# A weight stream of an expert stage: which entries are fetched aside, and where the shared expert stands

## The chip, the cores and the metric

The kernel runs on one core of a Trainium2 chip. The metric is the device time of one execution in microseconds, as the median of several runs. The core has five engines with queues of their own: TensorE (PE; matmuls, and weight loads as PEld), VectorE (DVE), ScalarE (ACT), GpSimd (POOL) and SyncE (SP), which here does nothing but issue transfers from device memory (HBM) into the on-chip memory and wait for their places to come free.

## The reference

Two transformer blocks run over 256 tokens of width 1024, in float32. The change touches the second half of the first block, a mixture of experts in four groups of eight, of which each token takes one group and in it two experts, with one shared expert for all tokens:

```python
def hier_moe(h, ...):
    t = h.reshape(-1, d)
    # combine: (tokens, 32) weights of the chosen experts, else 0
    ...
    a = jnp.einsum('nd,edf->nef', t, w_gate)       # w_gate, w_up: (32, 1024, 256)
    b = jnp.einsum('nd,edf->nef', t, w_up)
    hid = jax.nn.silu(a) * b * combine[:, :, None]
    routed = jnp.einsum('nef,efd->nd', hid, w_down)     # w_down: (32, 256, 1024)
    shared = (jax.nn.silu(t @ w_sh_gate) * (t @ w_sh_up)) @ w_sh_down
    return (routed + shared).reshape(bsz, slen, d)
```

Before it come a norm, an attention and convolution mixer with its output projection, and another norm. After it comes the second block: pooling, windowed attention, an output projection and a dense feed-forward part.

## The kernel before

**The stream.** All large weights lie in one array, `stream`, as entries of 128 x 2048 float32 (1024 KB each). SyncE fetches them in the order in which TensorE uses them. There are 14 entries for the mixer (0 to 13), then group 0 (entries 14 to 37), the shared expert's gate, up and down matrices (38, 39, 40), group 1 (41 to 64), group 2 (65 to 88), group 3 (89 to 112), and then the second block. (`entry_at` turns this order of use into the order in the array.) A group has `PAIRS` = 2 halves of four experts, and a half has 12 entries: eight for gate and up (`gate_up`), and four for down (`down`).

**Places.** An entry's place is as a rule one of the `SLOTS` = 8 places of `ring`, used in turn. Seven entries, those from `ASIDE_AT` = 20 to 26, are fetched aside instead, into room that stands empty at that time: five into the end of `work` (free when attention and convolution are done), and two into `turned_w` (free when the mixer's output projection is done). `ring_number(n)` is an entry's number among the ring's own, so entry 27 is number 20. With eight ring places and seven aside, fifteen entries, 14 to 28, can be on the chip before the expert stage has used any.

**Giving places back.** TensorE raises the semaphore `used` once for each entry it has passed, ring or aside. The raise hangs on the first matmul of a later step: the next entry's, the transposes of the hidden activations after the eighth gate and up entry, or `scatter`. SyncE's queue is strictly in order. For a ring entry it works out `gone`, the entry that held the place before, and waits for `used` to reach `gone + 1`; what is queued behind that wait waits too. Since 20 to 26 free no ring place, entry 34 takes the place of 19 and entry 35 that of 27:

```python
gone = ring_number(n) - SLOTS
if gone >= ASIDE_AT:
    gone += ASIDE
```

**The expert stage on TensorE.** `moe_group` gathers up to 32 tokens for each expert of the group by matmuls with a selection matrix (32 matmul records of 128x128 by 128x256), then for each half runs `gate_up`, `turn_hidden` (behind ScalarE's silu and VectorE's product), and `down`. The results of a half are scattered back into four PSUM banks by `scatter`: for half 0 that is after the second entry of half 1's `gate_up`, for half 1 at the group's end. Matmuls of an expert use 32 columns of the array, and four experts' run beside one another. An entry is eight matmul records. Groups 0 to 2 are written out, group 3 is the body of a loop which the data may repeat; here it ran once.

**The shared expert** runs after group 0, over all 256 tokens: `shared_gate_up` (64 matmul records of 128x128 by 128x256 over two entries), ScalarE's silu and VectorE's product (`shared_silu`, `shared_hidden`), `shared_turned` (four transposes and a copy), and `shared_down` (16 records of 128x128 by 128x512 with one entry), which adds to the same PSUM banks as `scatter`. Its down entry is given back by the first gather matmul of group 1 (`after_shared`).

The steps' lines are helpers' lines in the profile: nearly all matmuls carry line 1320, and are told apart by what they read.

Of the kernel before, what the change touches and what calls it, by code (L numbers as in the profile page):

```python
# [24 lines left out]
P = 128  # L25
D = 1024
DT = D // P
TOK = 256
# [32 lines left out]
B1 = 17  # L61
# [7 lines left out]
MOE_AT = B1 - 3  # L69
SHARED_AT = MOE_AT + MOE_GROUP  # L70
ASIDE_AT, ASIDE, ASIDE_WORK = 20, 7, 5
ASIDE_FROM = WORK - ASIDE_WORK * SLOT
# [43 lines left out]
def two_blocks(nc, x, meta, consts, small, gains, positions, stream, out):  # L116
    ctx = ExitStack()
    with ctx:
# [176 lines left out]
        def is_aside(n):  # L295
            return ASIDE_AT <= n < ASIDE_AT + ASIDE

        def ring_number(n):

            return n if n < ASIDE_AT else n - ASIDE  # L300

        def home(n):

            if not is_aside(n):
                return ring[:, ring_number(n) % SLOTS, :]
            i = n - ASIDE_AT
            if i < ASIDE_WORK:
                return work[:, ASIDE_FROM + i * SLOT:ASIDE_FROM + (i + 1) * SLOT]
            return turned_w[:, (i - ASIDE_WORK) * SLOT:(i - ASIDE_WORK + 1) * SLOT]

        def slot_ready(eng, n):

            if is_aside(n):
                eng.wait_ge(full2[n - ASIDE_AT], 16)
            else:
                eng.wait_ge(full[ring_number(n) % SLOTS], 16 * (ring_number(n) // SLOTS + 1))
# [117 lines left out]
        def _(sp):  # L434
# [3 lines left out]
            sp.dma_start(vec[:], small).then_inc(const_in, 16)  # L438
            for n in range(B1 + LOOPED * MOE_GROUP):
                if is_aside(n):  # L440

                    if n == ASIDE_AT:
                        sp.wait_ge(s["o_ps"], 2 * HEADS)
                        sp.wait_ge(s["convg_done"], CT)
                    if n == ASIDE_AT + ASIDE_WORK:
                        sp.wait_ge(s["mix_ps"], 2 * NT)
                    sp.dma_start(home(n), stream[entry_at(n)]).then_inc(full2[n - ASIDE_AT], 16)
                    continue
                gone = ring_number(n) - SLOTS
                if gone >= ASIDE_AT:  # L450
                    gone += ASIDE
                if 0 <= gone < Q_SLOT:
# [34 lines left out]
        def _(act):  # L487
# [178 lines left out]
            for g in range(LOOPED):  # L666
                moe_group(g)
                if g == 0:
                    shared_silu()
# [193 lines left out]
        def _(dve):  # L863
# [336 lines left out]
            for g in range(LOOPED):  # L1200
                moe_group(g, rankp[:, :, g * PER_GROUP:(g + 1) * PER_GROUP],
                          rankp[:, :, (g + 1) * PER_GROUP:(g + 2) * PER_GROUP], g == 0)
                if g == 0:
                    shared_hidden()
# [113 lines left out]
        def _(pe):  # L1318
# [292 lines left out]
            def shared_down():  # L1611
                slot_ready(pe, SHARED_AT + 2)
                pe.wait_ge(s["hst_sb"], 1)
                for i in range(NT):
                    for n in range(2):
                        for f in range(2):
                            last = mm(ps[:, 2 * i + n, :], hs[:, f, i * P:(i + 1) * P],
                                      home(SHARED_AT + 2)[:, f * D + n * 512:f * D + (n + 1) * 512], False, False,
                                      skip_group_check=True)

            def moe_group(it, g, moe_slot, freed, first=False, after_shared=False):

# [4 lines left out]
                for t in range(DT):  # L1627
                    for i in range(NT):
                        begin = mm(ps[:, gather_bank(t), (t % 2) * TOK:(t % 2 + 1) * TOK], xh[:, i, t * P:(t + 1) * P],
                                   sel[:, i, :], t % 2 == i == 0, False, skip_group_check=True)  # L1630
                        if after_shared and t == i == 0:
                            begin.then_inc(freed, 1)
                if first:
# [87 lines left out]

            def first_slot(k):

                slot_ready(pe, MOE_AT + k)
                return home(MOE_AT + k)

# [8 lines left out]
            for g in range(LOOPED):  # L1735
                moe_group(g, g, moe_slot(g) if g else first_slot, used, g == 0, g == 1)
                if g == 0:
                    shared_gate_up()
# [317 lines left out]
```

## Time and profile before

| | |
|---|---|
| median of 3 runs | 743.07 us (741.06 to 743.9) |
| the profiled execution's own time | 743.77 us |
| its span, first to last instruction | 741.9 us |
| granted TensorE clock, mean | 0.947 of full |
| PE busy | 662.8 us (89% of the span) |
| DVE, ACT, POOL busy | 334.6, 280.4, 42.9 us |
| read from HBM | 180.48 MB, 245 GB/s over the span |

The page cuts the span into 40 slices of 18.5 us. Of these, slices 7 to 20 hold the first block's end and the expert stage. Times in all rows are microseconds from the start of the span. In a timeline a row gives the start, the duration, the engine, the line, the operation, what is written and read, the count of records merged into it, and in brackets how long the engine stood idle just before and what ended that. A busy time alone says little: whether TensorE or the stream sets the pace differs between stages, so stretches are read one at a time.

### The profile page before, as it was taken

The page shows a single profiled execution, that of the slowest core. Times are in us where ns is not written, and L with a number is a line of the kernel's source. Part 1 is how long each engine was busy: PE and PEld are TensorE (multiplying, and loading weights), DVE is VectorE, ACT ScalarE, POOL GpSimd, SP SyncE. Part 2 cuts the span into 40 slices and gives each one's busy share as a digit, 9 for nine tenths or more (in the row PEclk, how much of TensorE's full clock was granted, in tenths as well). Part 3 has the DMA queues.
Part 4 walks back from the last instruction along what each step waited for, and adds up shares of the span by engine and source line. Part 5 has one row for each costly group of instructions (what it writes and reads, how often), then busy time and mean ns, then how long its engine had stood idle before and what let it go on. Part 6 is the DMA issues. An engine that isn't in the chain of part 4 may idle for free.

```text
span 741.9 us, 10752 instructions
## 1 busy us (share of the span) xinstructions
PE 662.8 (89%) x4431; PEld 516.6 (70%) x4431; DVE 334.6 (45%) x606; ACT 280.4 (38%) x521; POOL 42.9 (6%) x63
## 2 busy tenths in 40 slices
PE   8999899997895777677678999999989999999996
PEld 5979787733641133042148999989789999999994
DVE  7677555621020102012057565638845554445554
ACT  6655562311010110011045565673545433344432
POOL 1000102000000000000026400000000000000000
PEclk9999999999999687698799999999999999999998
DMA  9925309589869999999995534335525545545201
GB/s 354 417 90 223 114 1 407 245 340 388 348 251 424 420 422 421 422 419 422 420 420 208 197 114 148 137 115 174 187 106 204 182 173 197 198 170 180 105 1 57
DMA packets 26144, 182.22 MB, mean 246 GB/s; under 512 B 3040, under 2 KB 3168, under 8 KB 4464
## 3 DMA queue, kind: packets, MB, share of 16 engines
q1 hardware_dynamic: 25344, 178.81, 61.5%
q10 hardware_dynamic: 752, 2.73, 0.9%
q8 instruction: 35, 0.57, 0.3%
q14 instruction: 13, 0.11, 0.0%
HBM read 180.48 MB, written 1.05 MB: 245 GB/s over the span
## 4 chain that ended last, share of the span: by engine, by line
PE 67%; DMA 18%; DVE 7%; ACT 4%; issue 2%; POOL 1%; SPq 0%; DVEq 0%; ACTq 0%; POOLq 0%
PE ps L1320 64%; DMA ring<-stream_dram 17%; PE ps L1323 3%; DVE ring_r L351 2%; ACT single L344 1%; DMA vec<-small_dram 1%; DVE work L1274 1%; ACT work L746 1%; POOL stat L781 0%; DVE work L1277 0%; DVE single L1196 0%; ACT single L663 0%; DVE work L1183 0%; POOL stat L788 0%; DVE work L1230 0%
## 5 line engine op out<-in xcount | busy, mean ns | idle before, releaser
L1320 PE MATMUL ps<-turned,single 128*128 128x256 f32 (+1 forms) x1312 | 239.9, 285 | 2.0 <-DVE turned L1293 1.2
L1320 PEld LDWEIGHTS ps<-turned,single 128*128 128x128 f32 x1312 | 202.9, 189 | 4.7 <-issue 2.3
L1320 PE MATMUL ps<-turned,ring_r 128*128 128x256 f32 (+1 forms) x656 | 185.3, 282 | 0.0
L351 DVE TENSOR_TENSOR ring_r<-ring,single 128x1024 fp32r<-128x1024 f32 x134 | 160.9, 1243 | 49.8 <-ACT single L344 49.6
L1320 PE MATMUL ps<-ring,work 128*32 128x512 f32 (+2 forms) x814 | 136.1, 680 | 39.9 <-DMA ring<-stream_dram 35.6
L344 ACT ACTIVATE single<-ring 128x1024 fp32r<-128x1024 f32 x134 | 133.8, 1050 | 1.8 <-DMA ring<-stream_dram 1.2
L1320 PEld LDWEIGHTS ps<-ring,work 128*32 128x32 f32 (+1 forms) x814 | 39.7, 128 | 121.2 <-DMA ring<-stream_dram 75.0
L1320 PEld LDWEIGHTS ps<-turned,ring_r 128*128 128x128 f32 x656 | 124.0, 189 | 0.0
L1320 PE MATMUL ps<-single,turned 128*128 128x512 f32 (+3 forms) x208 | 60.1, 367 | 2.8 <-DVE turned L1007 1.8
L1320 PE MATMUL ps<-work 128*128 128x128 f32 (+5 forms) x272 | 55.7, 407 | 3.4 <-DVE work L877 1.8
L1320 PE MATMUL ps<-single 128*128 128x512 f32 (+1 forms) x257 | 51.2, 355 | 7.6 <-DVE single L1196 6.5
L1320 PE MATMUL ps<-single,work_r 128*128 128x512 f32 x176 | 56.4, 392 | 0.0
L1320 PEld LDWEIGHTS ps<-single 128*128 128x128 f32 x257 | 41.3, 198 | 20.6 <-DVE single L1196 10.9
L1320 PEld LDWEIGHTS ps<-work 128*128 128x128 f32 (+1 forms) x272 | 35.5, 190 | 12.6 <-issue 8.8
L1320 PEld LDWEIGHTS ps<-single,turned 128*128 128x128 f32 (+1 forms) x208 | 36.6, 183 | 9.2 <-issue 3.0
L765 ACT ACTIVATE work<-ps 128x256 f32<-128x256 f32 x22 | 8.5, 385 | 89.9 <-PE ps L1320 89.9
L657 ACT ACTIVATE work<-ps 128x256 f32<-128x256 f32 x8 | 3.1, 384 | 103.6 <-PE ps L1320 103.6
L1323 PE MATMUL ps<-cst,work 128*128 128x128 f32 (+2 forms) x174 | 28.6, 283 | 14.1 <-DVE work L1187 8.8
L781 POOL TENSOR_SCALAR stat<-stat 128x1 f32<-128x1 f32 (+1 forms) x13 | 5.7, 438 | 585.5 <-ACT work L678 249.3
L1297 DVE TENSOR_TENSOR work<-work,ps 128x256 f32<-128x256 f32 x22 | 9.3, 421 | 66.0 <-ACT work L765 66.0
L1323 PEld LDWEIGHTS ps<-cst,work 128*128 128x128 f32 (+2 forms) x174 | 20.9, 143 | 25.3 <-DVE work L1187 15.2
L1320 PEld LDWEIGHTS ps<-single,work_r 128*128 128x128 f32 x176 | 33.0, 188 | 7.0
(226 smaller groups left out, 599.0 us busy)
## 6 DMA issues: line engine op xcount, KB each, us to landing
ring<-stream_dram SPq DMA_DIRECT2D x161, 1024.0 KB, 12.1
work<-stream_dram SPq DMA_DIRECT2D x5, 1024.0 KB, 13.0
turned_w<-stream_dram SPq DMA_DIRECT2D x2, 1024.0 KB, 10.8
gain<-gains_dram ACTq DMA_DIRECT2D x3, 512.0 KB, 8.6
cst<-consts_dram ACTq DMA_DIRECT2D x1, 1066.0 KB, 9.0
h<-x_dram SPq DMA_DIRECT2D x2, 512.0 KB, 3.9
out_dram<-work SPq DMA_DIRECT2D x4, 256.0 KB, 2.0
vec<-small_dram SPq DMA_DIRECT2D x1, 451.5 KB, 5.9
```

What stands on the lines that cost most here:

```text
L344: act.activation(w_hi[k % HIGHS][:, a], ring[:, place, a], ACT.Copy).then_inc(s["whi_done"], 1)
L351: dve.tensor_tensor(ring_r[:, place, a], ring[:, place, a], w_hi[k % HIGHS][:, a].bitcast(F32), ALU.subtract).then_inc(s["wlo_done"], 1)
L657: act.activation(sg, ps[:, 4, 0:FF], ACT.Silu).then_inc(s["sg_done"], 1)
L746: act.activation(gate[:, m, :], gate[:, m, :], ACT.Sigmoid).then_inc(s["sig_done"], 1)
L765: act.activation(fsg[:, m % 4, :], ps[:, 4 + m % 4, 0:TOK], ACT.Silu).then_inc(s["fsg_done"], 1)
L781: pool.tensor_scalar(ms, ss, 1.0 / n, EPS, ALU.mult, ALU.add).then_inc(s["pool_step"], 1)
L1274: dve.tensor_tensor(gate[:, m, :], gate[:, m, :], ps[:, 2 + m % 4, :], ALU.mult).then_inc(s["br_sb"], 1)
L1297: dve.tensor_tensor(fh[:, m % 4, :], fsg[:, m % 4, :], ps[:, 4 + m % 4, TOK:2 * TOK], ALU.mult).then_inc(s["fh_sum"], 1)
L1320: return pe.matmul(o, lhsT, rhs, start=start, stop=stop, **kw)
L1323: return pe.transpose(o, a, ident[0:rows, 0:rows])
```

## The change

Three things are different. First, the seven entries fetched aside are now 15, 17, 19, ..., 27, every second one of the first fifteen of the stage, so ring and aside take turns; the ring holds 14, 16, ..., 28, and 29 on. SyncE's order of early fetches is written out: six ring entries (14 to 24), the five aside into `work` (15 to 23), the ring entries 26 and 28, and then the two aside into `turned_w` (25 and 27). Second, the shared expert stands behind group 1 (`SHARED_GROUP` = 2) on all engines and in the stream: group 1 is now entries 38 to 61, the shared expert 62 to 64, and group 2 begins at 65 as before. Third, the shared down entry is given back by the last matmul of `shared_down`, not by the first gather matmul of the next group.

```diff
-SHARED_AT = MOE_AT + MOE_GROUP
-ASIDE_AT, ASIDE, ASIDE_WORK = 20, 7, 5
+SHARED_GROUP = 2
+SHARED_AT = MOE_AT + SHARED_GROUP * MOE_GROUP
+ASIDE, ASIDE_WORK = 7, 5
+ASIDE_END = MOE_AT + 2 * ASIDE + 1
...
         def is_aside(n):
-            return ASIDE_AT <= n < ASIDE_AT + ASIDE
+            return MOE_AT <= n < ASIDE_END and (n - MOE_AT) % 2 == 1
+
+        def aside_number(n):
+            return (n - MOE_AT) // 2
 
         def ring_number(n):
 
-            return n if n < ASIDE_AT else n - ASIDE
+            return n if n < MOE_AT else n - ASIDE if n >= ASIDE_END else MOE_AT + (n - MOE_AT) // 2
+
+        def ring_entry(r):
+
+            return r if r < MOE_AT else MOE_AT + 2 * (r - MOE_AT) if r <= MOE_AT + ASIDE else r + ASIDE
...
-            for n in range(B1 + LOOPED * MOE_GROUP):
+            odd = range(MOE_AT + 1, ASIDE_END, 2)
+            order = list(range(MOE_AT)) + list(range(MOE_AT, MOE_AT + 2 * 6, 2)) + list(odd[:ASIDE_WORK])
+            order += [MOE_AT + 12, MOE_AT + 14] + list(odd[ASIDE_WORK:]) + list(range(ASIDE_END, B1 + LOOPED * MOE_GROUP))
+            for n in order:
                 if is_aside(n):
 
-                    if n == ASIDE_AT:
+                    if n == odd[0]:
                         sp.wait_ge(s["o_ps"], 2 * HEADS)
                         sp.wait_ge(s["convg_done"], CT)
-                    if n == ASIDE_AT + ASIDE_WORK:
+                    if n == odd[ASIDE_WORK]:
                         sp.wait_ge(s["mix_ps"], 2 * NT)
-                    sp.dma_start(home(n), stream[entry_at(n)]).then_inc(full2[n - ASIDE_AT], 16)
+                    sp.dma_start(home(n), stream[entry_at(n)]).then_inc(full2[aside_number(n)], 16)
                     continue
-                gone = ring_number(n) - SLOTS
-                if gone >= ASIDE_AT:
-                    gone += ASIDE
+                gone = ring_entry(ring_number(n) - SLOTS)
...
             for g in range(LOOPED):
                 moe_group(g)
-                if g == 0:
+                if g == SHARED_GROUP - 1:
                     shared_silu()
...
                                       home(SHARED_AT + 2)[:, f * D + n * 512:f * D + (n + 1) * 512], False, False,
                                       skip_group_check=True)
-
-            def moe_group(it, g, moe_slot, freed, first=False, after_shared=False):
+                last.then_inc(used, 1)
+
+            def moe_group(it, g, moe_slot, freed, first=False):
...
-                        begin = mm(ps[:, gather_bank(t), (t % 2) * TOK:(t % 2 + 1) * TOK], xh[:, i, t * P:(t + 1) * P],
-                                   sel[:, i, :], t % 2 == i == 0, False, skip_group_check=True)
-                        if after_shared and t == i == 0:
-                            begin.then_inc(freed, 1)
+                        mm(ps[:, gather_bank(t), (t % 2) * TOK:(t % 2 + 1) * TOK], xh[:, i, t * P:(t + 1) * P],
+                           sel[:, i, :], t % 2 == i == 0, False, skip_group_check=True)
...
-                moe_group(g, g, moe_slot(g) if g else first_slot, used, g == 0, g == 1)
-                if g == 0:
+                moe_group(g, g, early_slot(g) if g < SHARED_GROUP else moe_slot(g), used, g == 0)
+                if g == SHARED_GROUP - 1:
                     shared_gate_up()
                     shared_turned()
                     shared_down()
```

VectorE's `shared_hidden` moves like ScalarE's `shared_silu`. `early_slot` only looks up the place and the semaphore of an entry by its number in the order of use.

## Rows read from the trace of the kernel before

**Rows 1.** The page: GB/s in 40 slices of 18.5 us, and the chain's shares.
```profile
GB/s 354 417 90 223 114 1 407 245 340 388 348 251 424 420 422 421 422 419 422 420 420 208 197 114 148 137 115 174 187 106 204 182 173 197 198 170 180 105 1 57
...
PE 67%; DMA 18%; DVE 7%; ACT 4%; issue 2%; POOL 1%; SPq 0%; DVEq 0%; ACTq 0%; POOLq 0%
```

**Rows 2.** Waits of TensorE, 215 to 376 us.
```profile
PE ps L1320 <- DMA ring<-stream_dram: 34.8, 31, 2.2
```

**Rows 3.** The page, DMA issues: entries of the stream into the ring.
```profile
ring<-stream_dram SPq DMA_DIRECT2D x161, 1024.0 KB, 12.1
```

**Rows 4.** Windows: busy times (us, instructions), TensorE's granted clock, DMA share, GB/s.
```profile
113.00:140.00 27.00, 25.97 (x134) 21.29 (x132) 16.88 (x44) 8.54 (x18) 6.01 (x9) 0.94 1.01 425
141.00:149.00 8.00, 6.89 (x62) 4.84 (x65) 5.36 (x17) 2.97 (x5) 0.00 (x0) 1.00 0.02 5
149.00:150.50 1.50, 1.50 (x20) 0.39 (x12) 0.73 (x5) 0.00 (x0) 0.00 (x0) 1.00 0.76 186
164.00:169.00 5.00, 5.00 (x40) 2.29 (x44) 0.00 (x0) 0.00 (x0) 0.00 (x0) 1.00 0.29 90
200.00:215.00 15.00, 15.00 (x90) 8.14 (x92) 1.38 (x2) 1.68 (x4) 0.00 (x0) 0.93 0.37 128
215.00:376.00 161.00, 113.39 (x688) 38.06 (x680) 20.04 (x45) 15.54 (x31) 0.00 (x0) 0.81 1.01 421
```

**Rows 5.** Timeline of TensorE's matmuls, 146.1 to 206.5 us.
```profile
146.26 5.36 PE L1320 MATMUL ps<-ring,work 128*32 128x512 f32 x48
...
156.88 4.48 PE L1320 MATMUL ps<-work 128*32 128x512 f32 x24 [0.52 <-issue]
161.14 1.93 PE L1320 MATMUL ps<-turned_w,work 128*32 128x512 f32 x16
...
163.86 2.11 PE L1320 MATMUL ps<-single 128*128 128x512 f32 x8
165.90 5.36 PE L1320 MATMUL ps<-ring,work 128*32 128x512 f32 x48
...
176.71 1.07 PE L1320 MATMUL ps<-ring,work 128*32 128x512 f32 x8 [0.77 <-DMA ring<-stream_dram]
179.40 2.11 PE L1320 MATMUL ps<-single 128*128 128x512 f32 x8 [1.62 <-DVE single L1196]
181.35 13.97 PE L1320 MATMUL ps<-ring,work 128*128 128x256 f32 x64
...
197.94 8.80 PE L1320 MATMUL ps<-ring,work 128*128 128x512 f32 x16 [0.87 <-DVE work L1169]
206.17 0.68 PE L1320 MATMUL ps<-single 128*128 128x256 f32 x1
```

**Rows 6.** Timeline of SyncE's DMA issues in narrow stretches between 124 and 213 us.
```profile
124.72 0.80 SPq L447 DMA_DIRECT2D turned_w<-stream_dram  x2
126.62 0.81 SPq L458 DMA_DIRECT2D ring<-stream_dram  x2
...
148.19 4.62 SPq L458 DMA_DIRECT2D ring<-stream_dram  x6
...
166.98 0.33 SPq L458 DMA_DIRECT2D ring<-stream_dram  x1
...
167.84 0.33 SPq L458 DMA_DIRECT2D ring<-stream_dram  x1
...
206.88 0.33 SPq L458 DMA_DIRECT2D ring<-stream_dram  x1
...
212.43 0.33 SPq L458 DMA_DIRECT2D ring<-stream_dram  x1
```

**Rows 7.** Windows cut to stretches at low granted clock.
```profile
198.60:202.00 3.40, 3.40 (x6) 1.34 (x5) 0.00 (x0) 0.00 (x0) 0.00 (x0) 0.50 0.68 282
239.50:253.20 13.70, 9.64 (x42) 1.45 (x42) 0.42 (x1) 0.77 (x2) 0.00 (x0) 0.50 1.01 420
318.00:321.40 3.40, 3.09 (x7) 2.48 (x8) 0.26 (x1) 0.00 (x0) 0.00 (x0) 0.51 1.02 424
```

More of the change, by code:

```diff
@@ L305, in home @@
                 return ring[:, ring_number(n) % SLOTS, :]
-            i = n - ASIDE_AT
+            i = aside_number(n)
             if i < ASIDE_WORK:
@@ L313, in slot_ready @@
             if is_aside(n):
-                eng.wait_ge(full2[n - ASIDE_AT], 16)
+                eng.wait_ge(full2[aside_number(n)], 16)
             else:
@@ L1720, in moe_group, with early_slot, ready @@
                 scatter(PAIRS - 1).then_inc(s["moe_done"], 1)
-            def first_slot(k):
-                slot_ready(pe, MOE_AT + k)
-                return home(MOE_AT + k)
+            def early_slot(g):
+                def ready(k):
+                    n = MOE_AT + g * MOE_GROUP + k
+                    slot_ready(pe, n)
+                    return home(n)
+                return ready
             def moe_slot(it):
@@ L1735, in _ @@
             for g in range(LOOPED):
-                moe_group(g, g, moe_slot(g) if g else first_slot, used, g == 0, g == 1)
-                if g == 0:
+                moe_group(g, g, early_slot(g) if g < SHARED_GROUP else moe_slot(g), used, g == 0)
+                if g == SHARED_GROUP - 1:
                     shared_gate_up()
```

## The prediction

> **What bounds the kernel now.** I began with the page's slices and its chain. GB/s stands near 420 in nine slices in a row, 12 to 20 (about 223 to 389 us), and the chain that ended last is 67% PE and 18% transfers into the ring [rows 1]. So there are two regimes: a TensorE one for most of the span, and the expert stage, where weights arrive one stream entry at a time. The reader is to see in the waits of 215 to 376 us that TensorE waited 34.8 us, 31 times, for the ring [rows 2], and in the windows that the transfers ran at 421 GB/s over all of that stretch [rows 4]. An entry is 1024 KB, 1.049 MB [rows 3], so one takes 1.049 / 421 = 2.49 us, while TensorE needs only 5.36 / 6 = 0.89 us for one (48 matmul records are six entries) [rows 5]. In this stage the end is therefore set by the last transfer: a microsecond in which the transfers stand still is lost, and nothing else is, until the shared expert.
>
> Next I looked for where they stand still. The windows give three places [rows 4]: 141 to 149 (5 GB/s), 164 to 169 (90 GB/s, so 5 x (1 - 90/421) = 3.9 us idle), and 200 to 215 (128 GB/s, 15 x (1 - 128/421) = 10.4 us idle). In each, SyncE waits for a ring place. At 141 all fifteen entries fetched ahead have landed, and the first place comes free when TensorE has passed entry 14: the issue of entry 29 is at 148.19 [rows 6]. Six issues follow in 4.62 us, one per 0.86 us, for places of 14 to 19. Entry 35 waits for the place of 27, because 20 to 26 lie aside and free nothing; it is issued at 166.98 [rows 6]. The third is the shared expert: TensorE works 13.97 us on two of its entries and 8.80 us on the third [rows 5], and the issues at 206.88 and 212.43 wait for its last entry and for group 1's first [rows 6].
>
> **The start-up of a transfer.** After the issue at 148.19 the window 149 to 150.5 moves 1.5 x 186 = 0.28 MB, which is 0.66 us at full rate [rows 4]; so a transfer issued into a still queue is as good as started at 149.84, 1.65 us later. Entries 29 to 34 then end at 149.84 + 6 x 2.49 = 164.8, and entry 35 starts at 166.98 + 1.65 = 168.6. The gap of 3.8 agrees with the 3.9 of the window.
>
> **Part 1, the order of the early fetches.** The first six ring issues and the first five aside wait for what they waited for. The two ring entries after them (26 and 28 now) come ahead of the two aside in `turned_w` (25 and 27 now), so the latter, queued behind them on SyncE, go out after 126.62 rather than at 124.72 [rows 6]. The transfers run at 425 GB/s from 113 to 140 [rows 4]: 27 us carry 10.9 entries in one unbroken run. The four in question are its last and fill 4 x 2.49 = 10.0 us, so what is ahead of them ends at 140 - 10.0 = 130.0 or later, and 126.62 + 1.65 = 128.3 is earlier. Nothing is lost; all fifteen land by about 141 and TensorE first touches one at 146.26 [rows 5]. Were that cover gone it would cost up to 1.9 us, but hidden by those 5 us again. Price 0.
>
> **Part 2, places freed in group 0.** TensorE's own times until 168 don't depend on transfers, so they can be kept. An entry's place is free about 1.05 us after the next entry's first matmul (entry 28: 165.90 + 0.89, issue of 36 at 167.84) [rows 5, 6]. New freeing order:
> - 29, 30, 31, 32 want entries 14, 16, 18, 20 passed: 148.2, 149.9, 151.6, 153.3 (two of the 0.86 steps each). Transfers are continuous until 149.84 + 4 x 2.49 = 159.8.
> - 33 wants 22 passed. 22 to 24 are the first three down entries, 4.48 / 3 = 1.5 us each from 156.88 [rows 5]: 158.4 + 1.05 = 159.4, start 161.1. Idle 1.3.
> - 34 wants 24 passed: 161.14 + 1.05 = 162.2, start 163.9 (33 ended at 163.6). Idle 0.3.
> - 35 wants 26 passed, which the scatter at 163.86 says: 164.9, start 166.6, end 169.1.
> - 36 wants 28 passed: 167.84 as before, start 169.5. Idle 0.4.
> Before, entry 36 started at 168.6 + 2.49 = 171.1. The gain is 171.1 - 169.5 = 1.6 us. In another form: one transfer (2.49) less one step of TensorE (0.86). It can't be more, since 28 is passed when it was passed before; the three entries that now go earlier fill a hole whose end is fixed.
>
> **Part 3, the shared expert a group later.** TensorE's work is the same: two runs of 13.97 and 8.80 us with their gaps, 24.8 us from 181.35 to 206.17 [rows 5]. What counts is where the transfers are when it begins. Before, TensorE had already caught up by the end of group 0: at 176.71 it waited 0.77 us for the ring [rows 5], and the shared expert begins 181.35 - 176.71 = 4.64 us after that entry. Entry 37 landed near 168.6 + 3 x 2.49 = 176.1. Now group 1 is the group in front. TensorE's work on a group is far below 24 x 2.49 = 59.8 us (group 0 took 35.1, from 146.26 to 181.35 [rows 5]), so at its end it hangs on its last entry in the same way, as groups 1 to 3 do now [rows 2]. Entry 61 lands at 174.5 + 59.8 = 234.3, the shared expert begins at about 239.5, and again eight places lie between it and the front of the stream. The hole of 10.4 us opens again, at about 258 to 273. The move itself gains 0. Its matmuls lie on the path there as they do here, and from the start of the first transfer behind the hole 40 entries follow rather than 64: 24 fewer, and 24 more in front.
>
> The increment for the shared down entry stands at its last matmul rather than at the next group's first; those are neighbours (8.80 from 197.94, 206.17), and the hole's end hangs on the later issue, 212.43 [rows 5, 6]. Price 0. `ring_entry`, `aside_number` and the waits' new constants are worked out while the program is built and add no instruction.
>
> **Sum.** -1.6 us. The profiled execution took 743.77 us for its span of 741.9; that would be 742.2. It is 0.7 above the median, 743.07, so for the median 741.4.
>
> **The clock, a rival with two ends.** The granted clock in the shared expert fell to 0.50 from 198.6 to 202.0 [rows 7]; its sixteen down matmul records took 8.80 us where the sixty-four half as long before them, at full clock, took 13.97, thus 16 x 2 x 13.97 / 64 = 6.98 at that pace [rows 5]. A stretch of 3.4 us at half clock costs 1.8 us here, and here it costs the end. Behind a waiting group the clock can be anything: 0.50 from 239.5 to 253.2, and from 318.0 to 321.4 just over a group's end [rows 7]. The Trainium skill ("TensorE: Matmul & The Clock Gate", section on HAM oscillation) says that a kernel whose matmuls wait for transfers falls back to half rate and starts each burst cold, which speaks against putting the shared expert behind a group that waits; by the rule alone the result would be the slower side of this rival. The trace agrees with its first half (0.81 mean clock from 215 to 376 [rows 4]), not with every burst starting cold.
> - B: the fall inside the shared expert is missed, and none comes at its start. -1.6 - 1.8 = -3.4, 739.7.
> - C, the other side: the shared expert begins at 0.50 and stays there for a stretch as long as 239.5 to 253.2, 13.7 us, half of which (6.9) is lost: -1.6 + 6.9 = +5.3, 748.4. One fall more gives only +0.2. It decides from 3.2 us of half clock, and is more than 0.5% from (3.7 + 1.6) x 2 = 10.6 us. Against it: 198.6 to 202.0 and 318.0 to 321.4 ended within 3.4 us once dense work ran.
>
> **Other rivals.**
> - D: the later place hides the shared expert's hole, as TensorE would have more transfers in hand: -1.6 - 10.4 = -12.0, 731.1. For it would speak a TensorE that was behind the stream at the end of group 0 and ahead later; the 0.77 us wait at 176.71 speaks against it.
> - E: the hole at 164 is only moved. Now 33 to 36 are issued one at a time, and if each paid its start-up alone, they would take 4.14 each from 159.4: 36 would start at 159.4 + 3 x 4.14 + 1.65 = 173.5, 2.4 us later than before. Bounds are thus +2.4 and -1.6. I take -1.6, since 34, 35 and 36 are each issued 1.3 to 1.5 us before the one ahead of them ends, nearly the whole start-up; the middle (0, no gain: 743.1) is this rival's likely form. By the skill's fit in "DMA: Bandwidth & Descriptors" (anatomy of one DMA, 2.0 us and bytes/436) a lone entry takes 4.4 us, an estimate; that would put 36 at 174.6.
>
> **Numbers.** 0.5% is 3.7 us, about what a measurement of this kernel can tell from no change. Chances: forecast (with its clock as before) 0.55, 741.4; B 0.17, 739.7, three tenths of it under 739.4; C and lesser forms of it 0.09, half over 746.8; D or part of it 0.05; E 0.14. Faster: 0.05 + 0.17 x 0.3 + 0.02 of spread = 0.12; slower: 0.05; same: 0.83. The three runs lie 2.8 us apart, 741.06 to 743.9, so the likeliest case alone reaches from 740.0 to 742.8. The range takes in B and E: 738.8 to 744.6.
>
> **What would show it.** Right: issues into the ring at 148.2, 149.9, 151.6, 153.3, 159.4, 162.2, 164.9, 167.8; window 164 to 169 well above 90 GB/s, with some 2 us of idle between 159 and 170 in its place; the 64 shared matmuls start at about 239.5; a hole of 10.4 us near 258 to 273; 421 GB/s elsewhere until about 374. Wrong: a shared start before 236 or after 241, a second hole much smaller than 10 us, waits on the ring in group 0, or a granted clock of 0.50 over most of 239 to 262.

## The result and the profile after

The changed kernel is slower: 745.44 us as the median of 20 runs (742.22 to 749.45) against 742.96 us for 20 of the kernel before (738.80 to 744.99). The ratio is 1.0036, 95% interval 1.0020 to 1.0053: some 2.7 us lost where 1.6 us was forecast as gained. The profiled execution took 747.48 us, its span is 745.7 us and its mean granted clock 0.936, 2.0 us above the median, so its details are read beside other profiles below.

The page of the changed kernel, the slices' GB/s (one slice is 18.6 us) and the chain's shares:

```profile
GB/s 359 419 89 212 113 42 425 223 361 421 422 421 421 338 200 423 422 420 421 420 421 123 197 139 122 162 113 171 174 112 191 202 171 185 207 172 178 106 1 56
...
PE 67%; DMA 18%; DVE 7%; ACT 4%; issue 2%; POOL 1%; SPq 0%; DVEq 0%; ACTq 0%; POOLq 0%
```

Against [rows 1] the dip of slices 10 and 11 has gone to slices 13 and 14. It is the hole of the shared expert, and in this execution it is larger than before, as windows of 30 us around it show. First the kernel before, then the changed one:

```profile
195.00:225.00 30.00, 25.38 (x156) 12.13 (x154) 5.89 (x14) 3.62 (x8) 0.00 (x0) 0.94 0.69 272
```

```profile
250.00:280.00 30.00, 26.71 (x152) 15.18 (x150) 5.36 (x14) 3.09 (x8) 0.00 (x0) 0.94 0.59 232
```

At a full rate of 421 GB/s that is 30 x (1 - 272/421) = 10.6 us of standstill before and 13.5 after. SyncE's ring issues in narrow stretches, for entries 29 to 36:

```profile
145.75 0.33 SPq L468 DMA_DIRECT2D ring<-stream_dram  x1
...
147.47 0.33 SPq L468 DMA_DIRECT2D ring<-stream_dram  x1
...
149.19 0.33 SPq L468 DMA_DIRECT2D ring<-stream_dram  x1
...
150.90 0.33 SPq L468 DMA_DIRECT2D ring<-stream_dram  x1
...
157.45 0.33 SPq L468 DMA_DIRECT2D ring<-stream_dram  x1
...
159.75 0.33 SPq L468 DMA_DIRECT2D ring<-stream_dram  x1
...
161.94 0.33 SPq L468 DMA_DIRECT2D ring<-stream_dram  x1
...
165.39 0.33 SPq L468 DMA_DIRECT2D ring<-stream_dram  x1
```

This execution came to the expert stage 2.44 us earlier (143.82 against 146.26). With that taken off, the forecast's times were 145.8, 147.5, 149.2, 150.9, 157.0, 159.8, 162.5 and 165.4. The order of giving places back is as it was read from the code, and the times agree within 0.6 us. TensorE, the same execution:

```profile
143.82 1.06 PE L1330 MATMUL ps<-ring,work 128*32 128x512 f32 x8
...
174.96 1.07 PE L1330 MATMUL ps<-ring,work 128*32 128x512 f32 x8 [1.42 <-DMA ring<-stream_dram]
...
234.58 1.06 PE L1330 MATMUL ps<-ring,work 128*32 128x512 f32 x8 [0.69 <-DMA ring<-stream_dram]
237.26 3.54 PE L1330 MATMUL ps<-single 128*128 128x512 f32 x8 [1.62 <-DVE single L1206]
240.64 13.97 PE L1330 MATMUL ps<-ring,work 128*128 128x256 f32 x64
...
257.23 8.80 PE L1330 MATMUL ps<-ring,work 128*128 128x512 f32 x16 [0.88 <-DVE work L1179]
265.47 4.38 PE L1330 MATMUL ps<-single 128*128 128x256 f32 x32
```

Three things differ from the forecast. The hole is 3 us larger. Entry 37 is reached 174.96 - 143.82 = 31.14 us after the first entry, where it was 30.45 before [rows 5] and 28.8 was forecast. The scatter in front of the shared expert took 3.54 us, not 2.11: half clock. Windows of the same trace:

```profile
150.00:151.00 1.00, 1.00 (x14) 0.18 (x3) 0.00 (x0) 0.01 (x1) 0.00 (x0) 1.00 0.82 180
158.00:159.50 1.50, 1.50 (x16) 0.59 (x12) 0.75 (x1) 0.25 (x1) 0.00 (x0) 0.84 0.82 191
164.00:169.00 5.00, 4.81 (x48) 1.21 (x40) 0.00 (x0) 0.09 (x1) 0.00 (x0) 1.00 0.99 377
255.00:275.00 20.00, 18.43 (x104) 9.55 (x108) 2.56 (x4) 1.80 (x5) 0.00 (x0) 0.91 0.40 145
275.00:376.00 101.00, 72.20 (x428) 22.37 (x420) 12.64 (x29) 9.55 (x19) 0.00 (x0) 0.78 1.01 422
370.10:383.70 13.60, 10.75 (x37) 4.57 (x30) 3.40 (x6) 2.86 (x5) 0.21 (x2) 0.50 1.02 422
394.00:397.40 3.40, 3.40 (x18) 3.40 (x17) 3.40 (x8) 3.36 (x9) 0.00 (x0) 0.50 0.13 52
```

At 150 to 151 the rate falls to 180 GB/s, though entry 30 had been issued at 147.47, ahead of the end of entry 29. The 191 GB/s at 158 to 159.5 lie where the forecast had 1.3 us of idle, as entry 33 was issued only at 157.45. The stretch 164 to 169 has gone from 90 to 377 GB/s, and from 275 the rate is full. The last two windows are the half clock around the end of the stage: that end, and not the stage, looks most unlike before. First the tail of the kernel before, then that of the changed one, from the last entry (112):

```profile
375.26 1.06 PE L1320 MATMUL ps<-ring,work 128*32 128x512 f32 x8 [1.41 <-DMA ring<-stream_dram]
377.94 10.27 PE L1320 MATMUL ps<-single 128*128 128x512 f32 x44 [1.62 <-DVE single L1196]
391.45 1.97 PE L1323 MATMUL ps<-cst,work 128*128 128x128 f32 x16 [3.24 <-DVE work L1230]
393.18 0.48 PE L1320 MATMUL ps<-turned,single 128*128 128x256 f32 x2
```

```profile
374.84 1.94 PE L1330 MATMUL ps<-ring,work 128*32 128x512 f32 x8 [0.54 <-DMA ring<-stream_dram]
378.39 12.77 PE L1330 MATMUL ps<-single 128*128 128x512 f32 x44 [1.62 <-DVE single L1206]
393.56 3.31 PE L1333 MATMUL ps<-cst,work 128*128 128x128 f32 x16 [2.41 <-DVE work L1240]
396.53 0.78 PE L1330 MATMUL ps<-turned,single 128*128 128x256 f32 x2
```

The rows are the last entry, the last scatter with the 36 idle products behind it, the second block's transposes, and its first product. From first row to last it is 17.92 us before and 21.69 after. The last entry itself came 0.42 us earlier in the span. TensorE stood idle longer in front of the transposes before (3.24 us, clock full) than after (2.41 us, clock half), so the length of that wait alone doesn't decide the clock.

### The profile page after: what moved, and what is told of

Same layout as the page of the kernel before. It is cut to its first block, busy times and chain, and to the rows that moved or that the text cites. A ratio compares the mean times of both kernels' runs of the same rounds, so it can differ in the third digit from the quotient of the medians.

```text
span 745.7 us, 10752 instructions
## 1 busy us (share of the span) xinstructions
PE 668.2 (90%) x4431; PEld 517.6 (69%) x4431; DVE 334.6 (45%) x606; ACT 280.5 (38%) x521; POOL 42.0 (6%) x63
## 4 chain that ended last, share of the span: by engine, by line
PE 67%; DMA 18%; DVE 7%; ACT 4%; issue 2%; POOL 1%; SPq 0%; DVEq 0%; POOLq 0%; ACTq 0%
PE ps L1330 64%; DMA ring<-stream_dram 17%; PE ps L1333 3%; DVE ring_r L360 2%; ACT single L353 1%; DMA vec<-small_dram 1%; DVE work L1284 1%; ACT work L756 1%; POOL stat L791 0%; DVE work L1287 0%; DVE single L1206 0%; ACT single L673 0%; DVE work L1193 0%; POOL stat L798 0%; DVE work L1240 0%
## 5 line engine op out<-in xcount | busy, mean ns | idle before, releaser
L1330 PE MATMUL ps<-ring,work 128*32 128x512 f32 (+2 forms) x814 | 142.8, 709 | 37.8 <-DMA ring<-stream_dram 32.8
L1330 PE MATMUL ps<-work 128*128 128x128 f32 (+5 forms) x272 | 53.5, 384 | 2.8 <-DVE work L887 1.8
```

The costliest lines, as they stand in the source:

```text
L1330: return pe.matmul(o, lhsT, rhs, start=start, stop=stop, **kw)
```

## The experiments

One profile of each kernel couldn't tell chance from effect, so this table puts the profiles side by side. All columns are differences of rows like those above: first entry (its time in the span), from it to entry 37, from it to the last entry's first matmul, the shared expert (its first matmul to the next gather), the tail as just defined, and from there to the end. Products are matmuls whose results are thrown away; "everywhere" is groups 1 to 3 and the shared expert's two waits.

| kernel | first entry | to entry 37 | to last entry | shared | tail | to the end |
|---|---|---|---|---|---|---|
| before | 146.26 | 30.45 | 229.00 | 24.82 | 17.92 | 348.72 |
| before, second and third profile | 143.75, 145.60 | 30.50, 28.86* | 229.10, 225.90 | 24.83, 23.13 | 17.92, 17.92 | 348.83, 348.88 |
| changed | 143.82 | 31.14 | 231.02 | 24.83 | 21.69 | 349.17 |
| changed, three more profiles | 145.62, 146.04, 144.14 | 29.92, 31.30, 29.52 | 231.41, 228.81, 227.20 | 24.83, 23.14, 23.13 | 20.07, 19.47, 21.02 | 349.90, 348.88, 349.84 |
| interleaved order only, twice | 145.91, 146.13 | 29.50, 29.50 | 226.47, 226.44 | 23.13, 23.13 | 19.53, 18.73 | 349.09, 351.20 |
| shared expert late only, twice | 146.19, 146.35 | 30.48, 29.84* | 231.82, 227.23 | 24.83, 23.13 | 20.45, 20.94 | 351.04, 349.88 |
| waits spaced only | 144.38 | 29.26* | 226.18 | 23.13 | 21.93 | 348.71 |
| changed, products in group 1 | 145.65 | 28.86* | 227.29 | 23.14 | 20.97 | 349.89 |
| before, products in groups 1 to 3 | 145.96 | 28.81* | 227.61 | 24.83 | 18.50 | 349.83 |
| changed, products everywhere | 145.46 | 29.21* | 227.83 | 23.08 | 19.48 | 348.83 |
| changed, shared expert behind group 2 | 143.99 | 30.91 | 232.70 | 24.83 | 18.60 | 349.74 |
| interleaved, products everywhere | 145.48 | 29.38* | 227.81 | 23.18 | 19.36 | 348.86 |
| before, products everywhere | 145.99 | 30.60 | 227.37 | 23.07 | 19.42 | 348.86 |
| changed, tail kept warm | 144.23 | 29.81 | 230.69 | 24.87 | 17.94 | 348.84 |
| interleaved, tail kept warm | 146.04 | 29.81 | 226.62 | 23.13 | 17.92 | 348.82 |

The star marks executions whose granted clock was full all the way from the first entry to entry 37. In the others it was 0.50 for 3.4 us over group 0's first down entries. Here is that stretch in the kernel before, then a window of its third profile, which had no such fall, and the same three down entries there:

```profile
157.60:161.00 3.40, 3.40 (x20) 1.08 (x16) 0.39 (x1) 0.69 (x1) 0.00 (x0) 0.50 1.02 429
```

```profile
144.00:180.00 36.00, 30.30 (x243) 13.08 (x243) 9.74 (x30) 7.25 (x13) 0.00 (x0) 1.00 0.83 338
```

```profile
156.21 2.78 PE L1320 MATMUL ps<-work 128*32 128x512 f32 x24 [0.52 <-issue]
```

They took 2.78 us rather than 4.48 [rows 5]. Such a fall makes entry 37 come 1.6 us later, the same kernel having 30.45 and 30.50 with it and 28.86 without. So this column is compared at like clock only. The shared expert's 24.8 and 23.1 us differ in the same way, in both kernels.

**The two halves, and the whole again (runs 1 to 3), and spaced waits (run 4).** The halves: in the changed kernel, `SHARED_GROUP = 1`; and

```diff
-            return MOE_AT <= n < ASIDE_END and (n - MOE_AT) % 2 == 1
+            return ASIDE_AT <= n < ASIDE_AT + ASIDE
```

with `ASIDE_AT = 20`, `aside_number`, `ring_number`, `ring_entry` and the order of fetches as before. The spaced waits, on the kernel before (entries 29 to 34 wait for 14, 16, ..., 24 to be passed, as in the interleaved order; that is none to five entries more than before):

```diff
                 elif gone >= 0:
-                    sp.wait_ge(used, gone + 1)
+                    sp.wait_ge(used, (2 * gone - MOE_AT if MOE_AT <= gone < ASIDE_AT else gone) + 1)
```

> The entries fetched aside are every second one, and the shared expert stays behind group 0. Transfer theory: entries asked for one at a time lose transfer time between them (in the changed kernel 180 GB/s at 150 to 151 and 191 GB/s at 158 to 159.5, where 421 is full rate), so from the first matmul on a stream entry to the one on entry 37 it takes 31.1 us as in the changed kernel, not the 30.5 of before; +0.7 us of time, ratio 1.001. Forecast's theory: 28.8 us for that stretch and -1.6 us, ratio 0.998, so that all of the loss lies in the moved shared expert. Clock-only theory: the stretch is as in the transfer theory, and the rest of the loss is by chance in either half.

> The aside entries are 20 to 26 as before, and the shared expert stands behind group 1. Transfer theory with clock: +2 us, ratio 1.0027, from matmuls at half clock where TensorE sets the pace (the scatter in front of the shared expert, its down part, the end of the expert stage); the hole in the transfers behind it stays 10.4 us. Forecast's theory with all of the loss here: +4.3 us, 1.006. If moving is free, 1.000.

> The changed kernel once more, beside its two halves and on the same chip. Ratio 1.0036 as measured before; the two halves add up to it (0.7 + 2.0 us), and its second profile says which of the half-clock stretches of the first come back: if the scatter in front of the shared expert and the matmuls after the expert stage again run at half clock, the clock is the move's price; if neither does, it was chance.

> The kernel before with nothing changed but what SyncE waits for ahead of entries 30 to 34: two entries more passed for each, which are the spacings of the interleaved order. All seven aside entries and all places are as before. Transfer theory: the same dips in GB/s come back beside the third and fifth issue though nothing lies elsewhere, so spacing alone makes them; entry 34 ends at about 167 rather than 164.8, entry 35 is issued at 166.98 as before and starts behind it at once, so the time is within 1 us of before (0.999 to 1.001). If the dips come from where entries lie (TensorE reading one memory while transfers write beside it), there are none here and the rate is 421 whenever a transfer runs.

Measured: interleaved order 1.0018 (0.9998 to 1.0038), late shared expert 1.0074 (1.0047 to 1.0101), the whole 1.0033 (1.0004 to 1.0062), spaced waits 1.0030 (1.0006 to 1.0054). The halves don't add up to the whole in these figures; the intervals are wide. The interleaved order's profile contradicts its time: its stage is shorter, not longer. TensorE there:

```profile
172.81 3.64 PE L1330 MATMUL ps<-ring,work 128*32 128x512 f32 x32 [0.47 <-ACT work L669]
...
178.07 2.11 PE L1330 MATMUL ps<-single 128*128 128x512 f32 x8 [1.62 <-DVE single L1206]
180.02 3.18 PE L1330 MATMUL ps<-ring,work 128*128 128x256 f32 x14
```

The four down entries run without a wait for the ring (32 records in one piece; before, the last waited 0.77 us [rows 5]), and the shared expert starts 34.11 us after the first entry (145.91) rather than 35.09. Neither my transfer theory (31.1 us to entry 37) nor the forecast's size holds there. Entry 37 came 29.50 us after the first entry with no wait for the ring at all, so at this clock TensorE's own work puts it no earlier, and the forecast's 28.8 was out of reach. In the kernel with spaced waits nothing lies elsewhere, yet the rate falls while transfers are on their way, so spacing alone makes the dips. First a window of that kernel, then the same stretch after the first entry in the kernel before:

```profile
150.00:154.00 4.00, 2.83 (x28) 1.60 (x20) 1.75 (x7) 0.38 (x1) 0.00 (x0) 1.00 0.99 360
```

```profile
151.90:155.90 4.00, 2.81 (x28) 1.58 (x20) 1.77 (x7) 0.38 (x1) 0.00 (x0) 1.00 1.01 426
```

Its stage is short too (226.18), as its clock fell neither in group 0 nor in the shared expert. At like clock its entry 37 came 0.4 us later than before (29.26 against 28.86). Its tail is 21.93, and it was slower (1.0030, where 0.999 to 1.001 was expected). That was the first sign that the tail follows neither half as such.

**Clock (runs 5 to 7) and place (run 8).** The edit that keeps TensorE busy, here for group 1:

```diff
+                def keep_warm():
+                    for _ in range(warm):
+                        mm(ps[:, 5, FF:2 * FF], xh[:, 0, 0:P], xh[:, 0, P:P + FF], True, True)
...
+                        if t >= 3:
+                            keep_warm()
                         w = moe_slot(p * Q_SLOTS + t)
...
+                            keep_warm()
                             w = moe_slot(p * Q_SLOTS + GU_SLOTS + 2 * n + j)
...
+                          warm=5 if g in (1,) else 0)
```

> The changed kernel with five products of 128x128 by 128x256 (0.14 us each at full clock, results thrown away) ahead of the fourth to eighth gate and up entries and of the down entries of group 1 alone, the group in front of the shared expert, where TensorE waits for transfers anyway. Clock theory: no half clock from the group's second half into the shared expert, the eight scatter records in front of it take 2.1 us rather than 3.5, and the step from the first matmul on entry 61 to the shared expert's first 4.7 us rather than 6.1; 1 to 2 us of the 2.7 lost come back, ratio 1.0015 to 1.002. Theory that the loss is in the transfers (the 16 parts of an entry land 1.5 to 2.5 us apart, which the group in front of the shared expert now has to wait out): clock recovers but the time stays at 1.003 or above.

> The kernel before with the same products in groups 1, 2 and 3. If half clock at the end of the expert stage costs what the profiles suggest (17.9 us from the last entry's first matmul to the second block's first product in one execution, 19.5 to 21.9 in five others), that stretch is 17.9 in the profile and the time falls by 1 to 2.5 us, ratio 0.997 to 0.9985. If clock in a group that waits for transfers costs nothing anywhere, 1.000.

> The changed kernel with the products in groups 1, 2 and 3 and six more at each of the two waits inside the shared expert. Clock theory: no half clock anywhere in the stage; the shared expert takes 23.1 us from first matmul to the next gather rather than 24.8, the scatter in front of it 2.1, and the end of the stage 17.9; against the changed kernel -1.4 -1.7 -2.5 = up to -5.6 us, ratio 0.996 to 0.999. Transfer theory: of this only the two parts that are not the move's (shared 1.7, end 2.5) come, which the kernel before could have as well, and the stretch from the first entry to the shared expert stays 1.5 us longer than 24 entries explain.

> The changed kernel with the shared expert behind group 2. Both theories of a price paid once, for standing behind any group that waits for transfers: as the changed kernel, 1.002 to 1.005. If every group ahead of the shared expert costs something (transfers falling further behind), about 1.006 or more. If the price came from the place right behind group 1 alone, 1.000.

Measured: 1.0047 (1.0024 to 1.0069), 1.0000 (0.9974 to 1.0027), 1.0025 (1.0006 to 1.0044), 1.0056 (1.0033 to 1.0079). With the products in group 1 alone the clock came back as expected; TensorE in front of the shared expert:

```profile
235.65 1.07 PE L1330 MATMUL ps<-ring,work 128*32 128x512 f32 x8 [0.65 <-DMA ring<-stream_dram]
238.34 2.11 PE L1330 MATMUL ps<-single 128*128 128x512 f32 x8 [1.62 <-DVE single L1206]
240.28 13.97 PE L1330 MATMUL ps<-ring,work 128*128 128x256 f32 x64
```

From entry 61 it is 4.63 us again, and the last entry comes after 227.29 us. But the time did not fall: the tail was still 20.97. My clock theory for the stretch in front of the shared expert explains rows of some profiles and not the mean loss. Products everywhere (run 7) gave the stage's clock as expected (scatter 2.14 us, shared expert 23.08), but a tail of 19.48 and 1.0025, where 0.996 to 0.999 was expected. Behind group 2 the shared expert cost as much or a little more; its scatter was at half clock too (3.66 us), and a price that grows with the groups isn't told apart from one paid once. Its tail was only 18.60, and its stage was the longest, 232.70: in that execution most of the loss was not in the tail.

**Sizes once more (runs 9 to 12).** The interleaved order with all products (run 9), the two halves again, and the kernel before with all products.

> Every second entry aside, the shared expert behind group 0, the products in groups 1 to 3 and at the shared expert's two waits. Landing theory (an expert group that waits for transfers waits for the last of the 16 parts of each entry, so the shared expert is cheap only behind group 0): the stretch from the first entry to the shared expert is 32.4 us (33.4 of before less 1.0), the shared expert 23.1, so last entry 3 us earlier than in the kernel before, ratio 0.997. If the interleaved order has a cost that no profile here has shown, 1.000.

> The interleaved order alone once more, for its size: the first look had ratio 1.0018 (0.9998 to 1.0038) while its profile showed the shared expert 1.0 us earlier after the first entry than before (34.1 against 35.1). Landing theory: 0.9985 to 1.000. If the loss of the change sits partly in this half: 1.001 to 1.002 again.

> The shared expert behind group 1 alone once more. First look 1.0074 (1.0047 to 1.0101), but the profile explains only 2.4 us: 97.15 us from the first entry to the shared expert, which is 35.09 and 24 entries (59.65) and 2.4, of these 1.5 from parts of an entry landing apart and 0.9 from half clock. Landing theory: 1.003 to 1.004. If 1.007 comes back, half the cost of the move is elsewhere.

> The kernel before with the products in groups 1 to 3 and at the shared expert's two waits. The products in the groups alone gave 1.000; if half clock in the shared expert's down part (24.8 us against 23.1) is what pays, 0.998 to 0.999 with 23.1 us in the profile. If the gain of the changed kernel with all products (1.0025 against 1.0036) came from the groups behind a moved shared expert, 1.000.

Measured: 1.0019 (0.9993 to 1.0045), 1.0015 (0.9987 to 1.0043), 1.0028 (1.0006 to 1.0051), 1.0003 (0.9979 to 1.0026). The late shared expert's second figure is far below its first; between them it costs something like 0.3 to 0.7%. The interleaved order's second profile repeated the first within 0.03 us up to the last entry, and its time again was no better than before. Run 9 missed its forecast of 0.997: the shared expert started 35.47 us after the first entry instead of 32.4, as the scatter in front of it took 3.62 us. So half clock there can come behind group 0 too. Products in the groups bring nothing: they left the tail at 19.4 (runs 9 and 12), as other half-clock stretches came in its place.

**More profiles (runs 13 to 16).** Both kernels as they are, two profiles each.

> The kernel before, second profile. If half clock in front of the shared expert is the move's: none between 165 and 195 us, the shared expert starts 4.6 us after the first matmul on entry 37, and 33.4 to 35.1 us after the first entry's. If chance: as often as with the moved one.

> The changed kernel, third profile. If half clock is the move's: again a step of 5.5 to 6.1 us from entry 61 to the shared expert and 96.8 to 97.2 us from the first entry. Landing part alone, clock by chance: 4.7 us and 94.6 to 95 us.

> As the second profile of the kernel before: 4.6 us from entry 37 to the shared expert; last entry 226 to 229 us after the first; 17.9 to 21.9 us from the last entry to the second block's first product.

> As the third profile of the changed kernel: last entry 227.3 us after the first if the clock stays up in front of the shared expert, 231 to 232 if it does not; 20.1 to 21.7 us from the last entry to the second block's first product if that tail belongs to the change, spread over 17.9 to 21.9 if not.

The step from entry 61 to the shared expert was 4.63 and 4.64 us in these two profiles of the changed kernel and 6.06 and 6.01 in the first two, so half clock there comes in some executions. The tail is what separates the kernels' profiles: 17.92 in three of three before, 19.47 to 21.69 in four of four after. In the third profile of the kernel before, the ring also shows how an entry can land late in a group that waits for it:

```profile
233.28 1.06 PE L1320 MATMUL ps<-ring,work 128*32 128x512 f32 x8 [1.02 <-DMA ring<-stream_dram]
237.25 1.94 PE L1320 MATMUL ps<-ring,work 128*32 128x512 f32 x8 [2.91 <-DMA ring<-stream_dram]
239.73 1.93 PE L1320 MATMUL ps<-ring,work 128*32 128x512 f32 x8 [0.55 <-DMA ring<-stream_dram]
```

One step is 3.97 us and the next 2.48, while the rate stays full (418 GB/s from 233.3 to 240). It was followed up in the trace's landing marks, of which each entry has 16, one for each part of the transfer; TensorE waits for the last. The first part of the entry came on time, the last 2.1 us behind it.

**The tail alone (runs 17 and 18).** `keep_warm` only in group 3, also ahead of its transposes and twice ahead of its last scatter, and 48 idle products behind it rather than 36; first in the changed kernel, then with `SHARED_GROUP = 1`.

> The changed kernel with products thrown away in the last group alone (five ahead of each entry from the fourth on and ahead of the transposes, ten ahead of the last scatter) and 48 instead of 36 behind the stage, which reach up to the second block's first transposes. Tail theory: 17.9 to 18.2 us from the last entry to the second block's first product rather than 20.6, and the time falls by some 2.5 us, ratio about 1.000 to 1.001. If the tail is by chance and the loss is in the stage: ratio stays 1.0035.

> The same products with the interleaved order alone (shared expert behind group 0). Tail theory: last entry 226.4 us after the first as in its two profiles (before: 228.0 on average), tail 17.9 to 18.2, so 1 to 1.6 us faster than the kernel before, ratio 0.998 to 0.9985, and faster than both kernels. If the interleaved order costs something that the tail does not hold: 1.000 to 1.0015.

Measured: 1.0002 (0.9980 to 1.0024) and 1.0001 (0.9978 to 1.0024). The tail of the changed kernel with it:

```profile
374.92 1.06 PE L1330 MATMUL ps<-ring,work 128*32 128x512 f32 x8 [0.63 <-DMA ring<-stream_dram]
375.92 1.46 PE L1330 MATMUL ps<-single 128*128 128x256 f32 x10
377.61 13.03 PE L1330 MATMUL ps<-single 128*128 128x512 f32 x56 [0.23 <-DVE single L1206]
391.14 1.97 PE L1333 MATMUL ps<-cst,work 128*128 128x128 f32 x16 [0.51 <-DVE work L1240]
392.86 0.48 PE L1330 MATMUL ps<-turned,single 128*128 128x256 f32 x2
```

17.94 us, with TensorE busy to within 0.5 us of the transposes, and the rest of the span back at 348.84. The loss is gone to within the interval, though this execution's stage was as long as ever (230.69). The same products in the kernel before were not run, so it isn't shown that only the changed kernel gains by them; its three profiles already had this tail. The second kernel's profile is the sum that the expectation hoped for (226.62 and 17.92, span 739.4), but its time isn't told apart from the kernel before, so no version here is shown to beat it.

## Why the prediction was wrong

In means over four profiles of the changed kernel and three of the one before: first entry 144.9 against 145.2, to the last entry 229.6 against 228.0, tail 20.6 against 17.9, to the end 349.4 against 348.8. That is +4.6 us of span; the 20 timed runs of each say +2.7. The profiled executions of the kernel before were 1.2 us faster than its median on average, those of the changed one 0.9 us slower. The shares are read with that in mind. When the parts of entries 37 and 61 landed, by the landing marks, in us after the first entry:

| profiles | first part of 37 | last part of 37 | its parts apart | parts of 61 apart |
|---|---|---|---|---|
| before, the two with the fall in group 0 | 30.04, 30.19 | 30.41, 30.46 | 0.37, 0.27 | |
| changed, all four, with the same fall | 28.71, 28.61, 29.11, 28.60 | 31.09, 29.88, 31.25, 29.03 | 2.38, 1.27, 2.14, 0.43 | 2.43, 2.91, 2.71, 1.86 |

- **What bounds the stage**: right. The ring waits, the three holes and their causes came where they were read.
- **The early fetches and Part 1**: right in the profile shown, where TensorE had no wait for the ring until entry 37.
- **Part 2, -1.6 us**: the transfers nearly did what was forecast, TensorE did not. The step that failed is taking an entry as landed at one moment, 2.49 us after the one ahead. The first part of entry 37 came 1.4 us earlier than before in the mean, the last part, for which TensorE waits, only 0.1. In the kernel before, the parts of entries 33 and 34 landed 1.8 us apart; then the transfers stood still, and those of entry 35 landed within 0.5 us. The new order filled that hole, and in three of four profiles the parts were still over 1 us apart at entry 37. Over all profiles with the fall, entry 37 came after 30.5 us in the old order (four) and 30.2 in the interleaved one (nine); without it, after 29.2 in both (three each). So the term measured -0.3 to 0 us at entry 37, and -1.0 at the shared expert in the two profiles of the interleaved order alone (34.11 against 35.09 and 35.14). Rival E's size, no gain, came; the transfers' 1.4 of 1.6 us leaves 0.2 to its cause, a start-up paid by each. A lone entry took 4.9 us (29) and 4.7 us (35) from its issue to its last part in the kernel before, not 4.14. The prediction's estimate of 4.4 us rests on a fit that the Trainium skill ("DMA: Bandwidth & Descriptors", anatomy of one DMA) gives for transfers issued by GpSimd; SyncE issues these.
- **A reading under Part 2**: the 4.48 us of three down entries were taken for TensorE's own pace. They hold 3.4 us at half clock; the third profile has 2.78. That the forecast issue times agreed within 0.6 us was luck, as the same fall came again.
- **Part 3, 0 us**: what failed is "it hangs on its last entry in the same way". The parts of entry 61, on which the shared expert now hangs, landed 1.9 to 2.9 us apart; those of entry 37 in the kernel before 0.3 to 0.5. From 37 to 61 it took 59.6, 61.3, 60.2 and 60.6 us, not 59.65; and from 61 on 5.3 us in the mean, not 4.64, with the scatter at half clock in two of four. Together +1.5. On the forecast's clock the shared expert started at 243.1, 243.5, 242.4 and 241.0, where 239.5 was forecast and later than 241 was named as a sign of being wrong. The shared expert itself took the same two lengths in both kernels (24.8 and 23.1). The hole behind it was 13.5 us in the execution shown, not 10.4; but from the next gather to the last entry it is 109.4 us, which with 59.65 for 24 entries is 169.1 as before, so the larger hole is the same delay and not one more.
- **The clock**: the rival was placed wrongly. It was put inside the shared expert, where nothing changed. The forecast held the end of the stage for fixed, a term put at nothing without a reason, and there the last scatter ran in part at half clock in all four profiles of the changed kernel, and the second block's transposes in three: +2.6 us, and +0.6 just behind. Keeping TensorE busy there and nowhere else took the ratio from 1.0036 (1.0020 to 1.0053) and 1.0033 to 1.0002 (0.9980 to 1.0024). The intervals overlap a little, so this points to the tail as the largest part of the loss and doesn't prove it; that it is all of it is not shown.
- **Rivals B, C, D**: the fall in the shared expert's down part came and went in both kernels alike; no long stretch covered it; no hole was hidden.

By the Trainium skill's rule on bursts after waits ("TensorE: Matmul & The Clock Gate", section on HAM oscillation, named in the prediction) the slower side was to be expected. The trace agrees in direction, but of the changed kernel's four profiles two show the scatter in front of the shared expert at half clock and two at full.

Open: why the tail is at full clock in three of three profiles of the kernel before. Its last group does the same work, waits for the same transfers and has the same mean rate. The kernel with five waits spaced in group 0, which changes nothing behind it, had a tail of 21.93, so the tail is not tied to the moved shared expert as such. That it answers to the timing at which the stage ends is likely and not shown. Also open is what drives an entry's parts apart, and whether the interleaved order gains anything in time: its two profiles at like clock say 1.0 us, its four timed runs, two of them with products, between -0.2% and +0.5%.

## What to carry to other kernels

A stage that waits for transfers hands its successor a TensorE at a clock that nobody planned. When such a stage is re-ordered, the price may fall due at its end, on work that the change doesn't touch, so follow the chain past the last transfer and try idle products in the gap there. A transfer has landed for its user when its last part has: in a long unbroken run of transfers, read the wait in front of each entry, not the mean rate alone. Before taking a duration for an engine's own pace, look at the granted clock over it. And with 1 to 3 us at stake, take three or more profiles of both kernels and compare stretch by stretch, at like clock, before naming a cause.

## What the hardware showed that was not expected

- 1 MB transfers issued 1.7 us apart, each ahead of the end of the one before, lost some transfer time: 180 GB/s over 150 to 151 in the execution shown. From the first part of entry 29 to that of entry 32 it took 7.45 to 8.22 us in twelve profiles of the interleaved order and 7.44 to 7.47 in all seven where the issues came 0.86 us apart.
- In a group that waits for every entry, one step of 3.4 to 4.0 us instead of 2.48 appears (3.97 above, and 3.59 and 3.38 in the two profiles of the interleaved order) at full rate. In the trace's landing marks the parts of an entry are 0.2 to 1.0 us apart after the transfers stood still and 1.3 to 3.5 us after such steps, and they mostly stay so until the transfers stand still again.
- Five idle products ahead of each entry of group 1 kept the granted clock full from 144 to 283 us in run 5, over a group at whose end it otherwise fell in every profile of the changed kernel, and the time did not move.
